# A fused two-block network on one core: setup loads and modulation reordered with fillers for TensorE; attention with long and short rows in turn, its first scores inside the last dense job

## The reference, cut to what matters

```python
mod = silu(c) @ w_ada + b_ada                      # c: one vector of 1024; 3072 outputs
shift, scale, gate = split(mod, 3)
h = rmsnorm(x, norm_g) * (1 + scale) + shift
proj = h @ w_in                                    # retention, SSD, attention inputs
ret = retention(rotary(rq), rotary(rk), rv) * silu(rg)
ssd = rmsnorm(ssd_scan(conv(xbc), dt) * silu(z), g)
s = q @ k.T * scale + F[t] - F[s]; causal mask     # attention: 8 heads of 64, 512 tokens
fox = (softmax(s) @ v) * silu(fg)
x = x + gate * (concat(ret, ssd, fox) @ w_out)
```

## Time and profile before

| | |
|---|---|
| median of 3 runs | 3245.23 us (3244.2 to 3250.93) |
| the profiled execution | 3239.83 us, span 3238.0 us |
| mean granted TensorE clock | 0.987 |
| PE busy | 3083.6 us, 95% |
| DVE, ACT, POOL busy | 1341.3, 947.4, 1248.8 us |
| first dense product | 59.45 us |
| attention of layer 0, last dense job evacuated to last product | 436.3 to 488.3 us |

### The profile page before, as it was taken

One profiled execution on the slowest core, in us unless ns is written; L12 is line 12 of the kernel. 1 busy time (PEld: TensorE's weight loads), 2 busy tenths in 40 slices (PEclk: granted clock), 3 DMA queues, 4 the chain that ended last, 5 costly groups with the idle time before them and its releaser, 6 DMA issues. The chain is left out here.

```text
span 3238.0 us, 40354 instructions
## 1 busy us (share of the span) xinstructions
PE 3083.6 (95%) x16100; PEld 2523.3 (78%) x16100; DVE 1341.3 (41%) x2025; ACT 947.4 (29%) x1679; POOL 1248.8 (39%) x400
## 2 busy tenths in 40 slices
PE   4999989999998999999989999999999998999998
PEld 4878977788887788887757888888888775788886
DVE  6557544836735122233366322232222337632223
ACT  3356443336544111102455211011110245421101
POOL 1423325323233454444341444444444434154442
PEclk9999999999999999999999999999999999999999
DMA  5323214322230222232210222232223221022222
GB/s 230 118 78 111 83 54 173 133 72 104 80 106 28 89 94 96 86 97 96 78 41 14 91 91 98 82 106 91 91 88 99 85 79 40 27 79 97 93 89 71
DMA packets 45865, 287.86 MB, mean 89 GB/s; under 512 B 5496, under 2 KB 6008, under 8 KB 18680
## 3 DMA queue, kind: packets, MB, share of 16 engines
q1 hardware_dynamic: 42624, 270.58, 23.7%
q10 hardware_dynamic: 3096, 15.27, 1.4%
HBM read 283.67 MB, written 2.16 MB: 88 GB/s over the span
## 5 line engine op out<-in xcount | busy, mean ns | idle before, releaser
L1882 PE MATMUL PS<-x_parts,w_parts 128*128 128x512 f32 x4224 | 961.0, 390 | 4.1 <-ACT x_parts L727 4.1
L1823 POOL TENSOR_TENSOR w_parts<-w_raw,w_parts 128x2048 fp32r<-128x2048 f32 (+1 forms) x152 | 644.5, 4240 | 811.1 <-DVE w_parts L1957 756.6
L1882 PEld LDWEIGHTS PS<-x_parts,w_parts 128*128 128x128 f32 x4224 | 793.3, 188 | 173.4 <-issue 4.9
L136 POOL TENSOR_TENSOR w_parts<-w_raw,w_parts 128x2048 fp32r<-128x2048 f32 (+1 forms) x98 | 449.4, 4587 | 964.2 <-ACT w_parts L127 930.1
L329 PE MATMUL PS<-x_parts,w_parts 128*128 128x512 f32 x2784 | 693.5, 395 | 13.6 <-POOL w_parts L136 4.6
L329 PEld LDWEIGHTS PS<-x_parts,w_parts 128*128 128x128 f32 x2784 | 519.5, 189 | 133.3 <-issue 18.7
L1923 PE MATMUL PS<-hidden_parts,w_parts 128*128 128x512 f32 x2112 | 482.9, 390 | 0.0
L1923 PEld LDWEIGHTS PS<-hidden_parts,w_parts 128*128 128x128 f32 x2112 | 396.1, 188 | 83.9 <-issue 1.9
L1964 DVE TENSOR_TENSOR ffn_buffers<-PS,ffn_buffers 128x512 f32<-128x512 f32 x88 | 60.9, 692 | 732.0 <-PE PS L1882 708.9
L332 PE MATMUL PS<-w_parts,x_parts 128*128 128x256 f32 x2304 | 294.3, 288 | 2.2 <-POOL w_parts L136 2.2
L332 PEld LDWEIGHTS PS<-w_parts,x_parts 128*128 128x128 f32 x2304 | 282.5, 193 | 15.2 <-issue 11.6
(11 more groups left out here) (393 smaller groups left out, 3157.5 us busy)
## 6 DMA issues: line engine op xcount, KB each, us to landing
w_raw<-in_w_gu SPq DMA_DIRECT2D x88, 1024.0 KB, 4.7
w_raw<-in_w_in SPq DMA_DIRECT2D x70, 1024.0 KB, 4.8
w_raw<-in_w_d SPq DMA_DIRECT2D x64, 704.0 KB, 4.0
w_raw<-in_w_out SPq DMA_DIRECT2D x24, 1024.0 KB, 4.7
m_all<-in_w_next SPq DMA_DIRECT2D x14, 1024.0 KB, 8.4
m_all<-in_w_gate SPq DMA_DIRECT2D x8, 1024.0 KB, 4.7
ssd_buffers<-decay_rows ACTq DMA_DIRECT2D x16, 512.0 KB, 4.4
m_all<-in_w_next ACTq DMA_DIRECT2D x2, 1024.0 KB, 11.7
```

The source lines that it names most:

```text
L136: pool.tensor_tensor(parts[:, self.slot(u), 1, 0:n], raw[:, self.slot(u), 0:n], parts[:, self.slot(u), 0, 0:n].bitcast(F32), ALU.subtract) ...
L1823: pool.tensor_tensor(WP[:, b, 1, 0:n], RAW[:, b, 0:n], WP[:, b, 0, 0:n].bitcast(F32), ALU.subtract).then_inc(self.low, 1)
L1882: return pe.matmul(PS[:, 2 * b + g, :], WP[:, slot(b), w, c:c + P], XS[:, x, k, :], start=start, stop=stop)
```

## The change

In the setup: positions go to ACT's queue, the constants directly behind `c_row`; weight unit 0 is sent before rows 4, unit 1 after the constants of the retention. DVE lowers unit 0 after rows 3, POOL waits for that and lowers only unit 1. The sign of the sines moves to after rows 1, `norm.invert` to after rows 4, the wait for the retention's constants behind `modulated`. ACT rounds unit 0 before the square root, unit 1 after it. PE issues 6 fillers before the sums, takes the sums tile by tile behind the squares, and issues 4 more fillers behind the spread.

In the attention: the steps go through row blocks 3 and 0 in turn (16 steps, rows of 512 and 128 keys), then 2 and 1 (384 and 256). The four outputs have a PSUM bank each. PE's order is score s+2, turn s, weigh s-1; scores 0 and 1 are issued inside the last dense job, before its k-tiles 3 and 6, and exponential 0 stands before that job's evacuation. The finish of two tiles is split into gate and product parts, at steps 18 to 21 and at the end. The 24 products of job `je + 1` go ahead of the transposes, which use banks 6 and 7.

```diff
 class Attention:
     def place(self, s):
-        o, h = divmod(s, self.heads)
-        return o, NT - 1 - o, h
+        o, r = divmod(s, 2 * self.heads)
+        return (NT - 1, 0, NT - 2, 1)[2 * o + r % 2], r // 2
+    def bank(self, i):
+        return (0, 3, 2, 1)[i]
...
     def tensor(self, pe):
-        self.score(pe, 0)
-        self.score(pe, 1)
         for s in range(self.steps):
-            self.turn(pe, s)
             if s + 2 < self.steps:
                 self.score(pe, s + 2)
+            self.turn(pe, s)
             if s >= 1:
                 self.weigh(pe, s - 1)
         self.weigh(pe, self.steps - 1)
...
             copy(s)
-            if s % self.heads == 1 and s > self.heads:
-                finish(s // self.heads - 1, NT - s // self.heads)
-        finish(NT - 1, 0)
+            at = s - 2 * self.heads - 2
+            if 0 <= at < 4:
+                (finish_gate, finish_tile)[at % 2](at // 2)
+        for n in (2, 3):
+            finish_gate(n)
+        for n in (2, 3):
+            finish_tile(n)
...
 class InputNorm:
     def sums(self, pe, sq):
-        pe.wait_ge(self.squared, KD)
-        for c in range(NT):
-            for k in range(KD):
+        keep_busy(pe, 2, 6)
+        for k in range(KD):
+            pe.wait_ge(self.squared, k + 1)
+            for c in range(NT):
...
         self.spread_inverse(pe, 2)
+        keep_busy(pe, 2, 4)
...
 # retention, POOL
+                if not l:
+                    pool.wait_ge(stream.low, 1)
                 stream.lower(pool, RAW, WP, streams.end_r + SLOTS)
...
 # scan_and_attend, PE
-                for j in range(jk + 2, je):
+                for j in range(jk + 2, je - 1):
                     proj.run(pe, j, tokens)
+                proj.run(pe, je - 1, tokens, {3: first_score(0), 6: first_score(1)})
                 pe.wait_ge(evacuated, je)
-                pe.wait_ge(s_fb, 2)
                 att.tensor(pe)
+                pe.wait_ge(att.taken, 2)
+                pe.wait_ge(stream.low, proj.jobs[je + 1][0] + 1)
+                for k_ in range(12):
+                    pe.wait_ge(parts.high, k_ + 1)
+                    for w_ in range(2):
+                        product(je + 1, k_, w_, 0, k_ == 0 and w_ == 0, False)
                 for f in range(NT):
                     if f == 0:
                         pe.wait_ge(att.taken, NT)
...
-                        last = pe.transpose(PS[:, 2 + f % 2, ...
+                        last = pe.transpose(PS[:, 6 + f % 2, ...
...
 # scan_and_attend, ACT
-                for j in range(jk + 2, je):
+                for j in range(jk + 2, je - 1):
                     evacuate(j)
+                att.exponential(act, 0)
+                evacuate(je - 1)
                 proj.after(je - 1, act)
                 att.scalar(act)
...
 # setup, SP
                 sp.dma_start(B.c_row, dr["c_row"]).then_inc(s_c, 16)
-                sp.dma_start(ring[:, 0, :], ada_rows(0, 0)).then_inc(s_nl[0], 16)
-                sp.dma_start(posi, dr["pos"]).then_inc(s_in, 16)
                 sp.dma_start(cst[:, :], dr["c0"]).then_inc(s_in, 16)
-                sp.dma_start(ring[:, 2, :], ada_rows(0, 2)).then_inc(s_nl[2], 16)
+                for u in (0, 2):
+                    sp.dma_start(ring[:, u, :], ada_rows(0, u)).then_inc(s_nl[u], 16)
+                stream.send(sp, RAW, 1)
                 for u in range(4, NEARLY):
...
-                    if u < 4 + SLOTS:
-                        stream.send(sp, RAW, u - 3)
                 sp.dma_start(spec[:, 0:C1N], dr["c1"]).then_inc(s_c1, 16)
+                stream.send(sp, RAW, SLOTS)
...
 # setup, ACT
+                act.dma_start(posi, dr["pos"]).then_inc(s_in, 16)
...
                 norm.square(act, B.squares)
+                stream.round(act, act.copy, RAW, WP, 1)
+                norm.root(act)
                 stream.round(act, act.copy, RAW, WP, SLOTS)
...
 # setup, DVE
-                for u in range(4):
+                for u in range(NEARLY):
                     rows(u)
-                dve.wait_ge(s_sin, 2)
-                link(dve.tensor_scalar(SIN, SIN, const("sign"), None, ALU.mult))
-                for u in range(4, NEARLY):
-                    rows(u)
-                    if u == NEARLY - 2:
+                    if u == 1:
+                        dve.wait_ge(s_sin, 2)
+                        link(dve.tensor_scalar(SIN, SIN, const("sign"), None, ALU.mult))
+                    if u == 3:
+                        stream.lower(dve, RAW, WP, 1)
+                    if u == 4:
                         norm.invert(dve)
                 dve.wait_ge(s_nu, 2 * NEARLY)
                 dve.wait_ge(s_par, 16)
-                dve.wait_ge(s_c1, 16)
                 modulated(dve, link).then_inc(s_mod, 1)
                 dve.wait_ge(s_mod, 1)
+                dve.wait_ge(s_c1, 16)
```

More of the change, by code:

```diff
@@ L373, in turn @@
             def turn(self, pe, s):
-                _, i, _ = self.place(s)
+                i, _ = self.place(s)
                 pe.wait_ge(self.prob, s + 1)
@@ L383, in weigh @@
             def weigh(self, pe, s):
-                o, i, h = self.place(s)
+                i, h = self.place(s)
                 pe.wait_ge(self.copied, s + 1)
-                if h == 0 and o >= 2:
-                    pe.wait_ge(self.taken, o - 1)
                 for t in range(i + 1):
-                    last = pe.matmul(PS[:, i % 2, h * FD:(h + 1) * FD], self.pt[:, s % 2, t * P:(t + 1) * P],
+                    last = pe.matmul(PS[:, self.bank(i), h * FD:(h + 1) * FD], self.pt[:, s % 2, t * P:(t + 1) * P],
                                      self.vf(h, t), start=(t == 0), stop=(t == i))
@@ L402, in tensor, with exponential, vector @@
                 self.weigh(pe, self.steps - 1)
-            def scalar(self, act):
-                for s in range(self.steps):
-                    n = (NT - s // self.heads) * P
-                    act.wait_ge(self.smax, s + 1)
-                    if s >= 2:
-                        act.wait_ge(self.turned, s - 1)
-                    act.activation(self.p[:, s % 2, 0:n], self.sm[:, s % 2, 0:n], ACT.Exp,
-                                   bias=self.nm[:, s:s + 1], scale=-1.0,
-                                   accum_out=self.rs[:, s:s + 1]).then_inc(self.prob, 1)
-            def vector(self, dve, finish):
+            def exponential(self, act, s):
+                n = self.width(s)
+                act.wait_ge(self.smax, s + 1)
+                if s >= 2:
+                    act.wait_ge(self.turned, s - 1)
+                act.activation(self.p[:, s % 2, 0:n], self.sm[:, s % 2, 0:n], ACT.Exp,
+                               bias=self.nm[:, s:s + 1], scale=-1.0,
+                               accum_out=self.rs[:, s:s + 1]).then_inc(self.prob, 1)
+            def scalar(self, act):
+                for s in range(1, self.steps):
+                    self.exponential(act, s)
+            def vector(self, dve, finish_gate, finish_tile):
                 def maximum(s):
-                    n = (NT - s // self.heads) * P
+                    n = self.width(s)
                     dve.wait_ge(self.scored, s + 1)
@@ L1207, in _, with first_score, score, product @@
                     proj.run(pe, jk + n, tokens, {2 * i + 1: turn_y(4 * n + i) for i in range(4)})
-                for j in range(jk + 2, je):
+                for j in range(jk + 2, je - 1):
                     proj.run(pe, j, tokens)
+                def first_score(s):
+                    def score(pe):
+                        if s == 0:
+                            pe.wait_ge(evacuated, je - 1)
+                            pe.wait_ge(s_fb, 2)
+                        att.score(pe, s)
+                    return score
+                proj.run(pe, je - 1, tokens, {3: first_score(0), 6: first_score(1)})
                 pe.wait_ge(evacuated, je)
-                pe.wait_ge(s_fb, 2)
                 att.tensor(pe)
+                def product(j, k_, w_, x_, start, stop):
+                    u, m = proj.jobs[j][0], proj.jobs[j][3]
+                    w = WP[:, stream.slot(u), w_, k_ * m:(k_ + 1) * m]
+                    return pe.matmul(PS[0:m, proj.bank(j), :], w, mixed_parts(x_, k_), start=start, stop=stop)
+                pe.wait_ge(att.taken, 2)
[4 more added lines that the diff above has]
+                        product(je + 1, k_, w_, 0, k_ == 0 and w_ == 0, False)
                 for f in range(NT):
@@ L1218, in _ @@
                     for i in range(NT):
-                        last = pe.transpose(PS[:, 2 + f % 2, i * P:(i + 1) * P], fox_g[:, i, f * P:(f + 1) * P], ident)
+                        last = pe.transpose(PS[:, 6 + f % 2, i * P:(i + 1) * P], fox_g[:, i, f * P:(f + 1) * P], ident)
                     last.then_inc(s_ft, 1)
-                def product(j, k_, w_, x_, start, stop):
-                    u, m = proj.jobs[j][0], proj.jobs[j][3]
-                    w = WP[:, stream.slot(u), w_, k_ * m:(k_ + 1) * m]
```

(8 more changed lines are left out.)

42 lines of the change are left out of this document (27 added, 15 removed).

## The result

Forecast: 3224.6 us, range 3213 to 3236, chance of faster 0.93. Measured: 3225.66 us (median of four runs, 3223.93 to 3227.38) against 3247.55 (3244.2 to 3250.93, measured beside it): ratio 0.9937, 95% interval [0.9924, 0.995], so 16 to 25 us faster. The profiled execution took 3227.3 us, its span is 3225.5.

The account below looks back on a forecast made before the run. PE was busy 95% of the span, so only its idle or low-clock stretches could shrink. Setup -11.1 and attention -9.5 (two layers of -4.75) gave -20.6 us: 3219.2 on the profiled execution, 3224.6 against the median, range 3213 to 3236.

Parts of the forecast that it names:

- Constants and dot products: Setup loads: constants land at 10 us instead of 19.0, and DVE's dot products start at 17.4.
- DVE's chain: Setup: dot products 21.1, sine sign 0.5, subtraction of unit 0 2.3, reciprocal 0.25; unhindered L696 at 42.2 instead of 57.89.
- POOL's subtraction: Setup: POOL subtracts unit 1 for 4.8 us and DVE loses about 4.6, bounds 0 and 4.8.
- forecast A: Whole kernel: POOL blocks DVE once and attention pairs take 3.18 us; total 3224.6, chance 0.52.
- B: Setup rival: POOL's subtraction costs nothing, -11.1 becomes -15.7 to -17.3; total 3219, chance 0.17.
- The setup's sum: Setup: L696 starts at 46.8, 11.1 us earlier; gain between 5 and 17.
- The warm start: Setup: fillers could spare the first 8 products a cold start worth 1.7 us; taken as nothing.
- Attention, start to last product: Per layer: last product ends at 486.7 against 488.3, -1.6 us, with pairs of 3.18 then 2.68 and two finishes +2.0.
- Behind it: After the attention's last product, per layer: finish hidden -1.9, transposes at full clock -1.0, warm products -0.25 us.
- Rival C: Attention: the alternation pays in full, 2.68 us a pair, 7 us less; total 3217.5, chance 0.11.
- Rival E: Attention: PE idles 0.5 in each first-half pair and the clock falls to 1.2 GHz; slower, up to 3259.8, chance 0.05.
- rival D: A part does nothing: setup bound by loads, or pairs at 3.6 to 3.8; 6 to 8 us less gain, 3232, chance 0.15.

Follow-up runs that it names:

- Experiments 4: Changed kernel, but VectorE itself subtracts weight unit 1 behind the low parts and GpSimd starts with unit 2: 3218.12 us, ratio 0.9912.
- experiment 6: Changed kernel without the ten fillers that the change adds in the setup: 3221.46 us, ratio 0.9922.
- experiment 10: Changed kernel with the first two scores and the first exponential behind the last dense job again: 3228.24 us, ratio 0.9958.
- experiment 7: Changed kernel with the attention's rows in the order of before (tiles 3, 2, 1, 0), all else kept: 3222.57 us, ratio 0.9916.
- experiment 9: Changed kernel with the 24 output products behind the 16 transposes again, the last finish uncovered: 3229.81 us, ratio 0.995.
- experiment 5: Changed kernel with four unused products before PE's wait for masked scores in steps 3 and 5 of the state-space outputs: 3218.44 us, ratio 0.9913.

## Why the prediction was right, point by point

- **Total.** 20.6 us forecast, 21.9 between the medians, 20.5 by the ratio. By the traces the stretches that the change touches gained 24 (14.7, 5.1 and 4.2), 3.4 more than forecast, all of it from the setup. That the median still came within 1.1 us of the forecast is luck: the gain in these stretches was underrated by 3.4, and the stage of the state-space outputs, where the forecast had nothing, differs by more than that between executions; the interval of 16 to 25 us holds 20.6 and 24 alike.
- **Constants and dot products.** Forecast at 10 and 17.4, measured 8.61 and 16.09. The order of the loads did what the rate argument said, 1.4 faster.
- **DVE's chain.** From the first dot product to an unhindered L696 24.8 forecast, 23.9 measured (40.03); the subtraction of unit 0 took 2.29 (2.3 forecast).
- **POOL's subtraction** (forecast A against B): it blocks once, and DVE lost 3.6 (4.33 for 0.74) where 4.6 was forecast. Experiments 4 and 6 settle it: it is that instruction, and the price is what is left of it when the victim comes, not the victim's own length. By the Trainium skill (SBUF — State Buffer, section "SBUF: two separate sides") a VectorE operation with two SBUF inputs and a GpSimd operation exclude each other, and the one that started first keeps the other out for its whole instruction; the trace agrees, 4.33 and 4.35 beside 4.55 and 4.53.
- **The setup's sum, -11.1, was mis-sized:** the second job came 14.7 earlier. Of the missing 3.6, 2.2 are the earlier loads and shorter chain (L713 unhindered at 40.03 for 42.2) and 1.0 is the hold, 3.6 for 4.6; together they are DVE's, whose low parts end 14.3 earlier (54.70 for 68.99). The last 0.4 are PE's, which started cold before, and now waits for the held low part and runs at the lower clock behind it. The warm start, which I had put at nothing, was worth nothing (experiment 6).
- **Attention, start to last product.** -1.6 forecast. From the first product behind the evacuation to the end it was 52.0 (436.3 to 488.3, around) and is 49.0; less 1.1 moved, -1.9. A pair in the first half took 3.24 (3.18 forecast), in the second 2.75 (2.68); the two finishes in between cost 1.3 where 2.0 was forecast.
- **Behind it.** -1.9 -1.0 -0.25 = -3.15 forecast. From the last product to the end of the transposes it was 5.3 and is 7.5, of which 5.5 are products brought forward: -3.2. Per layer -5.1 in both together, where -4.75 was forecast; the whole stretches say -5.1 and -4.2.
- **What the terms did not say.** The loop took 48.0 us before and after; all of the -1.6 lay in the start, and experiment 10 puts the early scores at 1.9. Rival C (pairs at 2.68) fell, at 3.24. But the forecast set a pair against PE's own work and never against the same rows in order: with the banks and the finishes of this change, the loop takes 2.1 less, of which 1.45 is not moved work (experiment 7), so the alternation is a loss. And the cover of the finish hides more than the 1.9 and 1.0 it was costed at (5.6 up to the end of the transposes), since the change itself leaves two tiles instead of one for the end: 4.12 idle without it (experiment 9).
- **Clock.** Rival E did not come: 1.00 through both halves of the attention, with pairs of the first half 0.56 over PE's own 2.68. Nor did rival D: constants at 8.61, pairs under 3.6. What was not in the forecast is the state-space stage, 4 to 6 us a layer, in which the kernel before differs from execution to execution. If both kernels fell low there equally often, the change would be worth the 24 us that the other stretches show, which the interval of 16 to 25 holds; whether they do was not settled.

## What to carry to other kernels

Before a trace becomes the base of a sum, look for stretches in it that the change doesn't touch but whose duration is luck: here one stage differs by 6 us a layer between executions of one kernel, as much as the term under discussion. Where PE idles two or three microseconds for another engine, unused products in the idle time can hold the clock: here they won 6 to 8 us in two layers though they ran 0.7 over the idle time. Ahead of a wait that comes anyway, as in the setup, they won nothing. When work is moved out of a stretch, take it off before the stretch is called faster. A reordering that ships with other edits deserves its own experiment: the alternation cost some 1.45 us a layer under cover of edits that gained 6 to 7.

## What the runs showed of the hardware that I had not expected

- A GpSimd subtraction of 2048 columns (4.5 us) stretches the VectorE operation that it catches to 4.3 to 4.4 us, whether that has 512 columns or 8 (0.74 and 0.17 unhindered), so 3.6 to 4.2 us are lost. VectorE did the same subtraction in 2.28 us, so handing it over cost more than doing it. The same holding recurs behind the second job in both kernels: at 63.30 GpSimd subtracts unit 2 for 4.88 us, and a product of the rotation that takes 0.69 (L965) takes 4.98.
- With the same instructions, 20 us of layer 0's stage had a granted clock of 1.00 in one execution (PE idle 2.0 ahead of step 3) and 0.83 in the next (idle 2.9; first and second trace of before). The length of the idle time does not decide alone: in experiment 9 PE idled 2.89 ahead of step 3 in both layers, and its products took 2.00 in layer 0 and 3.67 in layer 1. With the idle time filled it was 1.00 in both windows of experiment 5.
- An unused 128x512 product in f32 takes 0.90 us at the full clock, as two instructions.
